# The eighth modulation slab ahead of projection slab 0, slab 0's lower half on GpSimd, and the first tiles scaled by two engines

## What is computed

```python
sc = jax.nn.silu(c)
mod = (sc @ p['ada_w'][l] + p['ada_b'][l])[:, None, :]
sh_m, sc_m, gt_m, sh_f, sc_f, gt_f = jnp.split(mod, 6, axis=-1)
h = _rmsnorm(x, p['pre_mix_g'][l]) * (1 + sc_m) + sh_m
...
proj = h @ w_in          # 1024 -> 4112: q, k, v, z and two gates
qkv, z, b_raw, a_raw = ...
conv = causal convolution of qkv over 4 rows, then silu
```

## Time and profile before

| | us |
|---|---|
| median of 3 runs | 1666.13 |
| lowest and highest run | 1662.53, 1666.99 |
| profiled execution | 1663.43 |
| its span, first to last instruction | 1661.6 |
| TensorE busy | 1574.3 (95%) |
| VectorE busy | 1146.5 (69%) |
| ScalarE busy | 958.3 (58%) |
| GpSimd busy | 105.4 (6%) |

### The profile page before, as it was taken

The page is one execution under the profiler, slowest core; times in us unless marked ns, Lnnn a source line. Parts: engine busy times, 40 slices in busy tenths (PEclk is TensorE's granted clock), DMA queues, the critical chain, the costliest instruction groups (busy, mean ns, idle before and its releaser), DMA issues.

```text
span 1661.6 us, 25552 instructions
## 1 busy us (share of the span) xinstructions
PE 1574.3 (95%) x10434; PEld 1325.5 (80%) x10434; DVE 1146.5 (69%) x1256; ACT 958.3 (58%) x1171; POOL 105.4 (6%) x193
## 2 busy tenths in 40 slices
PE   5999889988999998999879999999999999999997
PEld 3999467768999997996847888888888888888885
DVE  2866541575444455446667888888888888888887
ACT  2553423555333445336747777777777777777775
POOL 2211000000000000000011010100201010000021
PEclk9999899998999999999989999999999999999999
DMA  9820886479552558359329999999999999999995
GB/s 316 248 85 2 310 311 207 148 243 244 152 150 92 168 180 299 102 189 361 120 83 323 358 367 385 359 386 363 381 372 365 381 358 385 363 373 363 370 377 193
DMA packets 268789, 450.05 MB, mean 271 GB/s; under 512 B 12772, under 2 KB 125629, under 8 KB 268657
## 3 DMA queue, kind: packets, MB, share of 16 engines
q1 hardware_dynamic: 264312, 433.72, 75.5%
q0 software_dynamic: 3632, 13.11, 2.0%
q10 hardware_dynamic: 720, 1.50, 0.3%
HBM read 423.78 MB, written 24.51 MB: 270 GB/s over the span
## 4 chain that ended last, share of the span: by engine, by line
PE 46%; DVE 2%; DMA 1%; ACT 1%; issue 0%; SPq 0%; DVEq 0%; ACTq 0%
PE bank L427 14%; PE bank L429 14%; PE bank L428 14%; PE bank L2735 1%; DMA slot_rows<-gate_rows_far 1%; DVE w_lo_late L2975 1%; PE bank L2708 1%; PE bank L2669 0%; PE bank L2719 0%; ACT w_hi_late L2827 0%; PE bank L2663 0%; DVE raw L3114 0%; DVE raw L3108 0%; DVE xT L3103 0%; PE bank L2794 0%
## 5 line engine op out<-in xcount | busy, mean ns | idle before, releaser
L2975 DVE TENSOR_TENSOR w_lo_late<-raw,w_hi_late 128x2048 fp32r<-128x2048 f32 x262 | 598.5, 2291 | 102.0 <-ACT w_hi_late L2827 100.2
L2827 ACT ACTIVATE w_hi_late<-raw 128x2048 fp32r<-128x2048 f32 x262 | 502.6, 1918 | 156.1 <-PE bank L429 155.2
L427 PE MATMUL bank<-w_hi_late,hg_hi 128*128 128x512 f32 (+1 forms) x768 | 292.4, 381 | 0.8 <-DVE w_lo_late L2975 0.8
L428 PE MATMUL bank<-w_lo_late,hg_hi 128*128 128x512 f32 (+1 forms) x768 | 289.4, 377 | 0.0
L429 PE MATMUL bank<-w_hi_late,hg_lo 128*128 128x512 f32 (+1 forms) x768 | 289.4, 377 | 0.0
L331 DVE TENSOR_TENSOR w_lo_main<-raw,w_hi_main 128x2048 fp32r<-128x2048 f32 (+1 forms) x50 | 112.4, 2249 | 89.3 <-ACT w_hi_main L323 89.3
L427 PEld LDWEIGHTS bank<-w_hi_late,hg_hi 128*128 128x128 f32 x768 | 144.6, 188 | 29.8 <-DVE w_lo_late L2975 1.2
L429 PEld LDWEIGHTS bank<-w_hi_late,hg_lo 128*128 128x128 f32 x768 | 144.6, 188 | 29.3
L428 PEld LDWEIGHTS bank<-w_lo_late,hg_hi 128*128 128x128 f32 x768 | 144.7, 188 | 28.0
L427 PE MATMUL bank<-w_hi_late,act_hi 128*128 128x512 f32 x352 | 142.1, 404 | 0.7 <-DVE w_lo_late L2975 0.7
L429 PE MATMUL bank<-w_hi_late,act_lo 128*128 128x512 f32 x352 | 139.6, 396 | 0.0
(11 more groups left out here) (528 smaller groups left out, 2758.8 us busy)
## 6 DMA issues: line engine op xcount, KB each, us to landing
raw<-in_moe_w_gate SPq DMA_DIRECT2D x88, 1024.0 KB, 7.3
raw<-in_moe_w_up SPq DMA_DIRECT2D x88, 1024.0 KB, 7.5
raw<-in_moe_w_down SPq DMA_DIRECT2D x88, 1024.0 KB, 6.3
ada_delta<-in_ada_w SPq DMA_DIRECT2D x32, 1024.0 KB, 7.9
raw<-in_gdn_w_in SPq DMA_DIRECT2D x16, 1024.0 KB, 10.2
slot_rows_far<-zero_row SPq DMA_DIRECT2D x1, 12288.0 KB, 38.9
raw<-in_ffn_w_gate SPq DMA_DIRECT2D x22, 512.0 KB, 4.4
raw<-in_ffn_w_up SPq DMA_DIRECT2D x22, 512.0 KB, 5.6
```

The lines of the kernel that those rows point to most:

```text
L427: pe.matmul(out, w_hi, x_hi, start=start, stop=False)
L428: pe.matmul(out, w_hi, x_lo, start=False, stop=False)
L2827: act.activation(k.w_hi[:, m % SPL, :], k.raw[:, k.slot(m), :], ACT.Copy).then_inc(k.hi_ready, 1)
L2975: dve.tensor_tensor(k.w_lo[:, m % SPL, :], k.raw[:, k.slot(m), :], k.w_hi[:, m % SPL, :], ALU.subtract).then_inc(k.raw_split, 1)
```

## The change

The eighth modulation slab is issued ahead of projection slab 0. Slab 0's halves are no longer made in the setup block: ScalarE makes the upper half as its first work in the projection block, and GpSimd makes the lower half, as its first work there; VectorE starts its own series of lower halves with slab 1 and waits there for GpSimd's to be counted. The scaling of the eight tiles is shared: VectorE does the prompt's 256 columns, ScalarE the sample's 64, one tile ahead of its `h_hi`; ScalarE waits for the coefficients and for its own scaling by semaphores. TensorE waits, in slab 0, also until VectorE has scaled the prompt's part one tile further.

```diff
@@ setup_phase, SP
-            for n in range(ADA_GROUP - 1):
+            for n in range(ADA_GROUP):
                 k.ada_load(sp, n)
-            k.load_through(sp, 0)
-            k.ada_load(sp, ADA_GROUP - 1)
             k.load_through(sp, 2)
@@ setup_phase, ScalarE
-            k.ahead_hi(act, 0)
             k.ada_act(act, 4)
@@ setup_phase, VectorE
-            k.ahead_lo(dve, 0)
             k.ada_dve(dve, 4)
             k.ada_dve(dve, 1)
+            k.next_lo = 1
@@ conv_phase, TensorE
+            def part_ready(kt):
+                pe.wait_ge(lo_done, lo0 + kt + 1)
+                pe.wait_ge(scaled, scaled0 + min(kt + 2, KT))
...
-                        lambda kt: pe.wait_ge(lo_done, lo0 + kt + 1), aside=gate_products)
+                        part_ready, aside=gate_products)
@@ conv_phase, ScalarE
-            for kt in range(KT):
-                act.wait_ge(scaled, scaled0 + kt + 1)
-                act.activation(h_hi[:, kt, :], h32[:, kt, :], ACT.Copy).then_inc(hi_done, 1)
-                if kt == KT - 2:
+            k.ahead_hi(act, n0)
+            act.wait_ge(coef_ready, coef0 + 1)
+            for kt in range(KT + 1):
+                if kt < KT:
+                    act.activation(h32[:, kt, TP:T], k.x_normed(kt, 1), ACT.Identity, scale=k.coef[:, kt, 1:2],
+                                   bias=shift[:, kt, 1:2]).then_inc(sample_scaled, 1)
+                if kt:
+                    act.wait_ge(sample_scaled, sample0 + kt)
+                    act.wait_ge(scaled, scaled0 + kt)
+                    act.activation(h_hi[:, kt - 1, :], h32[:, kt - 1, :], ACT.Copy).then_inc(hi_done, 1)
+                if kt == KT - 1:
                     k.ahead_hi(act, n0 + 1)
@@ conv_phase, VectorE
-            run(dve.tensor_tensor(k.coef[:], k.coef[:], k.gain("pre_mix").unsqueeze(2).to_broadcast([P, KT, 2]), ALU.mult))
+            dve.tensor_tensor(k.coef[:], k.coef[:], k.gain("pre_mix").unsqueeze(2).to_broadcast([P, KT, 2]), ALU.mult).then_inc(coef_ready, 1)
+            dve.wait_ge(coef_ready, coef0 + 1)
             for kt in range(KT + 1):
                 if kt < KT:
-                    for s, (c0, n) in enumerate(STREAMS):
-                        last = dve.tensor_scalar(h32[:, kt, c0:c0 + n], k.x_normed(kt, s), k.coef[:, kt, s:s + 1],
-                                                 shift[:, kt, s:s + 1], ALU.mult, ALU.add)
-                    last.then_inc(scaled, 1)
+                    dve.tensor_scalar(h32[:, kt, 0:TP], k.x_normed(kt, 0), k.coef[:, kt, 0:1], shift[:, kt, 0:1],
+                                      ALU.mult, ALU.add).then_inc(scaled, 1)
                 if kt:
                     dve.wait_ge(hi_done, hi0 + kt)
                     dve.tensor_tensor(h_lo[:, kt - 1, :], ...).then_inc(lo_done, 1)
+            dve.wait_ge(k.raw_split, n0 + 1)
             k.ahead_lo(dve, n0 + AHEAD - 1)
@@ conv_phase, GpSimd
+            k.split_lo(pool, n0)
             for t in range(QKV_T):
```

More of the change, by code:

```diff
@@ L1001, in conv_phase @@
     scaled, scaled0 = k.sig["scaled"].sem, k.sig["scaled"].take(KT)
+    sample_scaled, sample0 = k.sig["times"].sem, k.sig["times"].take(KT)
+    coef_ready, coef0 = k.sig["coef"].sem, k.sig["coef"].take(1)
     with nc.sbuf_tensor("xp", [P, 4, T + 6], F32) as xp, nc.sbuf_tensor("conv_acc", [P, 2, T + 3], F32) as acc, \
```

## The result

The changed kernel's median is 1670.91 us (12 runs, 1667.52 to 1677.37) against 1666.56 for the kernel before beside it (12 runs): ratio 1.0035, 95% interval 1.002 to 1.0049. The forecast was 1665.7 in a range of 1661.0 to 1669.5. By the ratio it is slower by some 5.8 us, by the medians by 4.4, where 0.4 us faster was forecast. The profiled execution of the changed kernel took 1671.0 us, span 1669.3.

What follows compares the result with a forecast made beforehand. The eighth modulation slab's arrival was taken to set the block's start and first matmul. Block 4.4 us earlier, bare halves making the first matmul 0.25 later, slab 1 0.4 earlier: 1665.7 us, range 1661 to 1669.5.

Steps and rivals of the forecast that it cites:

- Part 1: Setup block: the eighth modulation slab lands earlier, its products end at 33.1, and the projection block starts at 35.3, 4.4 us earlier.
- The turn: TensorE's turn of the copied modulation products before the block: 0.94 us at full clock; half clock adds up to 0.9.
- Part 2: Projection block's start: slab 0's halves lose their cover; GpSimd starts at 37.35, takes 4.4 us and ends at 41.8.
- Part 3: VectorE's first h_lo subtraction waits for GpSimd's whole instruction, so the first matmul is at 42.45, 0.25 us later.
- Part 4: Shared scaling: VectorE's step per tile falls from 1.11 to about 0.8 us; slab 1's lower half is ready 0.95 us earlier.
- The sum: Slab 1 starts at 52.2 instead of 52.65, and this 0.4 us carries to the kernel's end: 1665.7 on the median's scale.
- the clock in slab 0: TensorE's clock during slab 0: 2.8 us more if it never returned, 2.9 us less if held at full.
- Slow GpSimd: Rival: GpSimd's lower half of slab 0 takes twice the expected time, 8.8 us, giving 1670; chance 0.12.
- a slab that doesn't come early: Rival: transfers share the engines, the eighth modulation slab still lands at 34.67, +4 us, again 1670; chance 0.06.

Runs made afterwards that it cites:

- the head held: Three unread 320-column matmuls added in TensorE's pauses ahead of the expert stage's 48 products: kernel before 1661.87 us (0.9979), changed kernel 1667.50 us (1.0005).
- lower half on VectorE: The changed kernel with slab 0's lower half made by VectorE instead of GpSimd: 1667.01 us, ratio 1.0012 to the kernel before.
- bare delay: The kernel before with three scratch fills, some 2 us, on VectorE between the coefficients and the first scaling: 1673.33 us, ratio 1.0058.
- in pieces: The changed kernel with late small transposes and slab 0's halves made piecewise by ScalarE and VectorE, none by GpSimd: 1662.63 us, ratio 0.9991 to before.

## Why the prediction was wrong

**Part 1, the block's start, is the step that failed.** It put the products' end at 33.1 and the block at 35.3, 4.4 us earlier. The block started at 37.25, 37.27, 38.95 and 38.93 in the four profiles with the changed setup (changed twice, changed with the head held, lower half on VectorE), on average 38.1, against 38.86 to 40.02 in six with the old one, on average 39.3. The gain is 1.2 us, not 4.4. The prediction read the 2.50 us of idle time at 34.67 and 24 records in 2.78 us as the rule. The two stand together in that one profile. In nine of the other thirteen the 32 records take 5.2 to 6.6 us without a pause, where they take 3.64 at full clock, and TensorE sets the end, with no wait for the slab. In the old order this cost little, since TensorE would else have waited for the eighth slab: its products end between 36.1 and 37.7 in all six profiles, with or without a wait. With the slab early, the slow products are on the path. In two of the four profiles of the changed setup they also start late, at 30.40 and 31.21 instead of 29.39, because TensorE's clock was low ahead of them. The turn did run at full clock, in 1.06 us (0.94 said).

**Part 2 was right**: GpSimd started 2.07 us after the block (2.05 said) and took 4.50 us (4.4 said). That the guess of two times 2.2 came so near is in part luck, as no row of the kernel before priced the second input. The Trainium skill's GPSIMD Engine Reference, section "Performance versus the Vector engine", gives 4497 ns; the trace agrees with its 4.50 us.

**Part 3 was right**: VectorE's first h_lo stood until GpSimd had ended. The lock of the Trainium skill, SBUF — State Buffer, section "SBUF: two separate sides", is thus seen in this case with GpSimd first as well as with VectorE first. From the block's start to the first matmul it was 6.98 us, 7.15 said.

**Part 4 was right in size**: VectorE's step per tile is 46.22 - 45.37 = 0.85 us (0.8 said). ScalarE's sample scaling took 0.39 us instead of 0.23 and hid.

**The sum failed twice.** The start lost 1.9 us by part 1 in the first profile (37.2 for 35.3) and 3.6 in two others, and so slab 1 was at 53.9, 53.6 and 55.7 in the three profiles of the changed kernel instead of 52.2. On average that is 2.3 us later than in three of the kernel before (one of the three with the head held in each case, which leaves the start as it is), where 0.4 us earlier was forecast: the 4.5 us by which the bare halves lengthen the way from the block's start to the first matmul (6.98 for 2.46) stand against a gain of 1.2, and slab 0 then takes some 0.8 us less. The second failure is the sentence that a shift of slab 1 carries on to the end one for one. The bare delay, with nothing of the change in it, cost several times its size, and part of that was the clock at the head of the expert stage. The prediction allowed for the clock in slab 0 only. Of the changed kernel's own loss the head accounts for some 1 us; the 5.8 us by which the first two profiles differ there overstate it.

**The rivals.** Slow GpSimd and a slab that doesn't come early were both not so; that the median lies near their 1670 is chance. The cause, TensorE as the bound of the setup block at its low clock, was named only as an end of 0.9 us for the turn.

**What stays open.** Slab 1's 2.3 us and the head's 1 leave some 2 us of the changed kernel's 5.3 to 5.8 without a place. Between slab 1 and the 48 products the profiles take 810 to 816 us, and one profile each can't say how much of that a kernel's median holds. Why the clock at the head of the expert stage was low in both profiles of the changed kernel and in the bare delay's, but in one of two of the kernel before, was not settled either; the rank counts ahead of the products, 8 columns wide, are the same in all, and so is the 0.66 us of idle time in those without the three matmuls.

## What to carry to other kernels

Before you take a wait for data away, ask what the engine behind it would take at its low clock, and read that from more than one execution: a wait that looks like the bound may be hiding a slow engine. A part that is moved out from under a wait is paid in full if nothing else covers it; in pieces, in the order of use, it costs a fraction (2.2 us from the block's start to the first matmul instead of 7.0). And where a kernel has a place whose clock may fall, a small shift ahead of it can cost several times its size, and two profiles can differ there by chance: hold the clock there first (three unread matmuls in pauses were worth 3.6 us to the kernel before by medians), then measure the small edits.

## What was not expected of the hardware

- The same program's 48 products and what follows took 25.13 us at a clock of 1.00 or 30.95 us at 0.78 in two executions.
- Three matmuls of 320 columns ahead of them gave 25.0 us in four of four profiles; without them it was five of ten.
- A delay of some 2.4 us at 40 us moved the median by 8 us; with the three matmuls in both kernels it moved it by 3.
